# A two-layer retention and gating trunk: constants in one packed load, weight loads held until a stage, value weights in halves, steps one place later

## The reference

```
xn = rmsnorm(h) * norm_g
q, k, v, g_r, u, v_g, g_g = split(xn @ w_in)               # 7 x 1024 columns, 8 heads of 128
o  = retention(rope(q), rope(k) * 128**-0.5, v)            # decayed, chunks of 128, state S per head
o  = groupnorm(o) * silu(g_r)
vn = layernorm(v_g) * ln_g + ln_b
s  = tril(ws[h]) @ vn (per chunk of 128) + bs[h]
m  = u * s * silu(g_g)
h  = h + concat(o, m) @ w_out
```

## Time and profile before

| | |
|---|---|
| median of 3 runs | 1325.68 us (1325.44 to 1326.54) |
| profiled execution | 1327.66 us |
| its span on the slowest core | 1326.1 us (cores: 1317.5 to 1326.1) |
| granted PE clock, mean of the cores | 0.989 to 0.993 |
| PE / PEld busy | 1206.9 / 611.7 us |
| DVE / ACT / POOL busy | 711.7 / 649.4 / 536.1 us |
| moved by DMA | 124.64 MB |

### The profile page before, as it was taken

One profiled execution on the slowest core, in us unless ns is written; L12 is line 12 of the kernel. 1 busy time (PEld: TensorE's weight loads), 2 busy tenths in 40 slices (PEclk: granted clock), 3 DMA queues, 4 the chain that ended last, 5 costly groups with the idle time before them and its releaser, 6 DMA issues.

```text
span 1326.1 us, 23218 instructions; the slowest of 8 cores (1317.5 to 1326.1 us)
## 1 busy us (share of the span) xinstructions
PE 1206.9 (91%) x7524; PEld 611.7 (46%) x7666; DVE 711.7 (54%) x1408; ACT 649.4 (49%) x1053; POOL 536.1 (40%) x528
## 2 busy tenths in 40 slices
PE   0159999999999999998999999999999999999997
PEld 0024445555555555544444444455555555554443
DVE  0024545766677676642233333567777666764333
ACT  1245734665656566553332343465656565563222
POOL 3001002776766677540002100476767667671000
PEclk9979999999999999999999999999999999999999
DMA  9941300523542452388339300054145315425432
GB/s 148 175 140 50 96 19 6 108 46 71 110 84 50 86 118 59 94 150 240 130 123 192 69 1 4 5 109 93 43 92 110 60 48 118 98 75 138 160 129 111
DMA packets 114934, 124.64 MB, mean 94 GB/s; under 512 B 15936, under 2 KB 89920, under 8 KB 113792
## 3 DMA queue, kind: packets, MB, share of 16 engines
q1 hardware_dynamic: 99840, 85.40, 21.8%
q0 software_dynamic: 14976, 37.76, 19.0%
HBM read 126.01 MB, written 34.87 MB: 121 GB/s over the span
## 4 chain that ended last, share of the span: by engine, by line
PE 77%; DVE 9%; SPq 5%; issue 4%; ACT 3%; DMA 1%; POOL 0%; DVEq 0%; ACTq 0%; POOLq 0%
PE ps L656 32%; PE ps L936 18%; PE ps L561 16%; SPq L464 5%; DVE B_k L670 1%; PE ps L895 1%; DVE tt L792 1%; PE ps L790 1%; DVE B_k L669 1%; PE ps L726 1%; PE ps L531 1%; PE ps L810 1%; PE ps L713 1%; PE ps L771 1%; ACT sq L454 1%
## 5 line engine op out<-in xcount | busy, mean ns | idle before, releaser
L454 ACT ACTIVATE B_q<-ps 64x512 f32<-64x512 f32 x128 | 75.7, 591 | 107.4 <-DVE A_q L681 100.9
L454 ACT ACT_TABLE_LOAD x65 | 83.4, 1283 | 37.2 <-DVE tt L792 28.7
L785 POOL TENSOR_TENSOR VO<-og,tt 128x512 bf16<-128x512 f32 x64 | 80.1, 1272 | 23.0 <-ACT tt L454 20.6
L672 POOL TENSOR_TENSOR kT_84<-A_k,B_k 128x512 bf16<-128x512 f32 x32 | 40.7, 1272 | 98.3 <-DVE B_k L670 95.6
L454 ACT ACTIVATE tt<-tt 128x1024 f32<-128x1024 f32 x64 | 67.7, 1057 | 3.6 <-ACT tt L454 0.4
L753 DVE SCALAR_TENSOR_TENSOR S_90<-S_90,ps 128x128 f32<-128x128 f32 x240 | 67.6, 282 | 3.1 <-DVE oS L912 0.4
L887 POOL TENSOR_TENSOR vmask<-eye_137,v_s 16x1024 bf16<-16x1024 f32 x32 | 60.4, 1886 | 18.5 <-PE ps L895 18.1
L621 POOL TENSOR_TENSOR xh_s<-xh_s,lng_s 16x1024 f32<-16x1024 f32 x2 | 4.7, 2336 | 149.3 <-ACT xh_s L454 149.3
L534 DVE TENSOR_TENSOR xnT<-ps,ngT_148 128x1024 bf16<-128x1024 bf16 x16 | 19.4, 1215 | 76.2 <-PE ps L531 39.6
L561 PE MATMUL ps<-wv_103,xnT 128*128 128x512 bf16 x249 | 59.8, 379 | 0.4
L561 PE MATMUL ps<-wv_104,xnT 128*128 128x512 bf16 x253 | 59.7, 379 | 0.2
(11 more groups left out here) (348 smaller groups left out, 3127.5 us busy)
## 6 DMA issues: line engine op xcount, KB each, us to landing
stt_109<-st SPq DMA_DIRECT2D x16, 512.0 KB, 4.1
stt_108<-st SPq DMA_DIRECT2D x16, 512.0 KB, 6.2
ss_out<-stt_108 SPq DMA_DIRECT2D x16, 512.0 KB, 3.3
ss_out<-stt_109 SPq DMA_DIRECT2D x16, 512.0 KB, 7.6
hb_50<-xp SPq DMA_DIRECT2D x8, 512.0 KB, 4.1
hb_51<-xp SPq DMA_DIRECT2D x8, 512.0 KB, 4.4
hb_52<-xp SPq DMA_DIRECT2D x8, 512.0 KB, 4.6
hb_53<-xp SPq DMA_DIRECT2D x8, 512.0 KB, 5.3
```

The costliest lines, as they stand in the source:

```text
L454: P.add("act", lambda e: e.activation(out=out, in_=in_, func=func, **kw), r, w, t_act(n) + (0.2 if "accum_out" in kw else 0), tset=tset)
L672: pool(lambda e: e.tensor_tensor(out=dst[:], in0=A_k[:], in1=B_k[:], op=ALU.add), A_k.k() + B_k.k(), dst.k(), 512)
L785: pool(lambda e: e.tensor_tensor(out=VO[:, h, s], in0=og[:, u.n % 2, :], in1=tt[:, u.n % 2, :], op=ALU.mult), og.k(u.n % 2) + tt.k(u.n % 2 ...
```

## The change

- norm_g, ln_g, ln_b of both layers and w00, b00 are packed by the host into the columns of `c_small` (100 columns instead of 20, one contiguous load); the ten element loads are gone.
- On SP, x chunk 0 is first, then the identity and `c_small`, then the sample rows and x chunks 1 to 3.
- `P.add` takes extra dependencies (`after`). The head weights of blocks 1 and 2 wait for the last value matmul recorded so far (`mark["v"]`).
- Each `wv` is loaded in two halves, and `v_mm` records its eight matmuls as two steps of four, each waiting for its half.
- The scale of a normed chunk goes from ACT to DVE.
- In the output stage of layer 0, `norm_back` comes two chunks behind instead of one, and the `wv` loads of layer 1 are recorded at chunks 5, 7, 9 and 11, each waiting for that chunk's last matmul, instead of all at chunk 2.
- KT is recorded ahead of ONE.
- Guessed durations: SM 0.064 to 0.056, ONE 0.218 to 0.42, `s_proj` 40 x 0.06 to 40 x 0.026, `s_o` 8 x 0.06 to 8 x 0.03.

```diff
-    def add(self, eng, fn, r=(), w=(), dur=0.1, semkey=None, tset=None, nbytes=0):
+    def add(self, eng, fn, r=(), w=(), dur=0.1, semkey=None, tset=None, nbytes=0, after=()):
...
+        for j in after:
+            deps[j] = 2
...
-    w_v = dt_in("w_v", [DEPTH, 4, 128, 8, 512])
+    w_v = dt_in("w_v", [DEPTH, 4, 2, 128, 4, 512])
...
-        ngT = [T("ngT%d" % i, [128, 8], F32) for i in range(2)]
-        lngT = [T("lngT%d" % i, [128, 8], F32) for i in range(2)]
-        lnbT = [T("lnbT%d" % i, [128, 8], F32) for i in range(2)]
-        w00 = T("w00", [128, H], F32)
-        b00 = T("b00", [128, H], F32)
+        sm8 = lambda i: small[:, 20 + 8 * i:28 + 8 * i]
+        ngT, lngT, lnbT, w00, b00 = ([sm8(5 * l + i) for l in range(2)] for i in range(5))
...
-        def w_item(l, item):
+        def w_item(l, item, after=()):
...
-                dma("pool", wv[i][:], w_v[l, i], [], wv[i].k(), wv[i].name, 2097152)
+                for k in range(0, 8, 4):
+                    dma("pool", wv[i][:, k:k + 4, :], w_v[l, i, k // 4], [], wv[i].k((k, k + 4)), (wv[i].name, k), 1048576, after=after)
...
-            act(x_ap, h_ap, AF.Copy, h_k + rst[i].k(), x_k, D, scale=rst[i][0:n, :])
+            dve(lambda e: e.tensor_scalar(out=x_ap, in0=h_ap, scalar1=rst[i][0:n, 0:1], scalar2=None, op0=ALU.mult),
+                h_k + rst[i].k(), x_k, D)
...
-            def mm(e):
-                for k in range(8):
-                    r = e.matmul(ps[:, b, :], xnT[:, k, c * 128:(c + 1) * 128], wv[i][:, k, :], start=(k == 0), stop=(k == 7))
-                return r
-            pe(mm, xnT.k(None, (c * 128, c * 128 + 128)) + wv[i].k(), [bk(b)], 8 * MM)
+            for k0 in range(0, 8, 4):
+                def mm(e, k0=k0):
+                    for k in range(k0, k0 + 4):
+                        r = e.matmul(ps[:, b, :], xnT[:, k, c * 128:(c + 1) * 128], wv[i][:, k, :], start=(k == 0), stop=(k == 7))
+                    return r
+                mark["v"] = pe(mm, xnT.k((k0, k0 + 4), (c * 128, c * 128 + 128)) + wv[i].k((k0, k0 + 4)), [bk(b)], 4 * MM)
...
             if l == 0:
                 dma("sp", h1[c * 128:(c + 1) * 128, :], h[:], h.k(), [("h1", c)], h.name, 524288)
+                if c >= 2:
+                    norm_back(1, c - 2)
                 norm_front(c)
...
         for c in range(4):
             x_load(0, c)
             if c == 0:
+                ld(identf, c_ident)
+                ld(small, c_small, 51200)
                 dma("sp", hs[:], xs_in, [], hs.k(), hs.name, 65536)
-                for l in range(DEPTH):
-                    dma("sp", ngT[l][:], norm_g[l].rearrange("(c p) -> p c", p=128), [], ngT[l].k(), ngT[l].name, 4096,
-                        allow_slow_non_contiguous=True)
...
                     for it in witems[wi:n0]:
-                        w_item(l, it)
+                        w_item(l, it, after=[mark["v"]])
...
+                KT(l, u)
                 if p:
                     ONE(l, p, pp)
-                KT(l, u)
...
-                    if l == 0:
-                        for i in range(4):
-                            w_item(1, ("v", i))
                 if c == 8:
                     s_out(l)
-                if l == 0 and c >= 1:
-                    norm_back(1, c - 1)
+                if l == 0 and c in (5, 7, 9, 11):
+                    w_item(1, ("v", (c - 5) // 2), after=[mark["o"]])
...
             if l == 0:
+                norm_back(1, NCH - 2)
                 norm_back(1, NCH - 1)
```

More of the change, by code:

```diff
@@ L22 @@
 NCORES = 8
+NSMALL = 100
 BLK = 64
@@ L413, in build_nc @@
         eye16 = T("eye16", [NS, NS], F32)
-        small = T("small", [128, 20], F32)
+        small = T("small", [128, NSMALL], F32)
         kinv = lambda h: small[:, h:h + 1]
@@ L450, in pe @@
         def pe(fn, r, w, dur):
-            P.add("pe", fn, r, w, dur)
+            return P.add("pe", fn, r, w, dur)
         def act(out, in_, func, r, w, n, tset=None, **kw):
@@ L461, in pool, with dma @@
             P.add("pool", fn, r, w, t_pool(n))
-        def dma(eng, out, in_, r, w, key, nbytes, **kw):
-            P.add(eng, lambda e: e.dma_start(out=out, in_=in_, **kw), r, w, semkey=key, nbytes=nbytes)
+        def dma(eng, out, in_, r, w, key, nbytes, after=(), **kw):
+            P.add(eng, lambda e: e.dma_start(out=out, in_=in_, **kw), r, w, semkey=key, nbytes=nbytes, after=after)
         def ld(t, src, nbytes=65536, **kw):
@@ L486, in w_item @@
                 t = wsl[slot_of[(l, h, g)]]
-                dma("pool", t[:], w_h[l, h, g], [], t.k(), t.name, 524288)
+                dma("pool", t[:], w_h[l, h, g], [], t.k(), t.name, 524288, after=after)
             else:
@@ L490, in w_item @@
                 t = wo2[wo_of[(l, j)]]
-                dma("pool", t[:], w_o[l, j], [], t.k(), t.name, 1048576)
+                dma("pool", t[:], w_o[l, j], [], t.k(), t.name, 1048576, after=after)
         slot_of, wo_of = {}, {}
@@ L549, in sample_norm @@
             dve(lambda e: e.tensor_tensor(out=sxT[:], in0=pb[:, 0:8 * NS].rearrange("p (k t) -> p k t", k=8),
[L550 to L551 removed]
+                                          in1=ngT[l].unsqueeze(2).to_broadcast([128, 8, NS]), op=ALU.mult),
+                small.k(), sxT.k() + [bk(b)], 128)
+        mark = {}
         vrot = Rot(range(6))
@@ L634, in sample_vg @@
             dve(lambda e: e.tensor_tensor(out=sT_s[:], in0=ps[:, b, 0:8 * NS].rearrange("p (k t) -> p k t", k=8),
[L635 to L638, removed]
+                                          in1=w00[l].unsqueeze(2).to_broadcast([128, 8, NS]), op=ALU.mult),
+                small.k(), sT_s.k() + [bk(b)], 128)
+            dve(lambda e: e.tensor_tensor(out=sT_s[:], in0=sT_s[:], in1=b00[l].unsqueeze(2).to_broadcast([128, 8, NS]),
+                                          op=ALU.add), sT_s.k() + small.k(), sT_s.k(), 128)
         prot = Rot([0, 1, 2])
@@ L789, in ONE @@
             b = brot()
-            pe(lambda e: e.matmul(ps[:, b, :], ones_r[:], sq[:], start=True, stop=True), ones_r.k() + sq.k(), [bk(b)], MM)
+            pe(lambda e: e.matmul(ps[:, b, :], ones_r[:], sq[:], start=True, stop=True), ones_r.k() + sq.k(), [bk(b)], 0.42)
             E = E_h[u.h % 2]
@@ L817, in GM @@
                                                  op0=ALU.mult, op1=ALU.add),
-                lngT[l].k() + Bc[h % 2].k(), s32.k() + [bk(b)], 512)
+                small.k() + Bc[h % 2].k(), s32.k() + [bk(b)], 512)
             g = sgg[u.n % 2]
@@ L839, in w_prep2 @@
                                                  op0=ALU.mult, op1=ALU.add),
-                lnbT[l].k() + gmb[0].k(), Bc[h % 2].k() + [bk(b2)], 128)
+                small.k() + gmb[0].k(), Bc[h % 2].k() + [bk(b2)], 128)
         sstate = {}
@@ L997, in build_nc @@
             if c == 0:
+                ld(identf, c_ident)
+                ld(small, c_small, 51200)
                 dma("sp", hs[:], xs_in, [], hs.k(), hs.name, 65536)
-                for l in range(DEPTH):
-                    dma("sp", ngT[l][:], norm_g[l].rearrange("(c p) -> p c", p=128), [], ngT[l].k(), ngT[l].name, 4096,
-                        allow_slow_non_contiguous=True)
         for i in range(4):
             w_item(0, ("v", i))
-        ld(small, c_small, 10240)
+        P.add("dve", lambda e: e.tensor_copy(identb[:], identf[:]), identf.k(), identb.k())
         ld(maskT, c_maskT)
@@ L1007, in build_nc @@
         for l in range(DEPTH):
[L1008 to L1013, removed]
             if l == 0:
@@ L1163 @@
     w_v = w7[:, :, :, [GCOL["v"], GCOL["vg"]], :].reshape(DEPTH, 8, 128, 2, 2, 512).transpose(0, 3, 4, 2, 1, 5)
-    w_v = w_v.reshape(DEPTH, 4, 128, 8, 512)
+    w_v = w_v.reshape(DEPTH, 4, 128, 2, 4, 512).transpose(0, 1, 3, 2, 4, 5)
     w_o = w_out.reshape(DEPTH, 8, 2, 128, 1024).transpose(0, 1, 3, 2, 4)
-    shared = dict(norm_g=f(norm_g), w_h=f(w_h), w_v=f(w_v), w_o=f(w_o), gm_ws=f(gm_ws), gm_b=f(gm_b), ln_g=f(gm_ln_g),
-                  ln_b=f(gm_ln_b), fin_g=f(final_g), c_small=_C["small"], c_E=_C["E"], c_rope=_C["rope"],
+    cols = lambda a: f(a).reshape(8, 128).T
+    rep = lambda a: np.repeat(f(a).reshape(1, H), 128, axis=0)
+    small = f(np.concatenate([_C["small"]] + [p for l in range(DEPTH) for p in (
+        cols(norm_g[l]), cols(gm_ln_g[l]), cols(gm_ln_b[l]), rep(f(gm_ws)[l, :, 0, 0]), rep(f(gm_b)[l, :, 0]))], axis=1))
+    shared = dict( w_h=f(w_h), w_v=f(w_v), w_o=f(w_o), gm_ws=f(gm_ws), gm_b=f(gm_b), ln_g=f(gm_ln_g),
+                  ln_b=f(gm_ln_b), fin_g=f(final_g), c_small=small, c_E=_C["E"], c_rope=_C["rope"],
                   c_maskT=_C["maskT"], c_ident=_C["ident"], c_eye16=_C["eye16"])
```

17 lines of the change are left out of this document (7 added, 10 removed).

## The result

The changed kernel takes 1271.6 us (median of 4, 1271.55 to 1271.8) against 1325.8 before: a ratio of 0.9591 (0.9574 to 0.9607), 54.2 us less. The forecast was 1257.5, with a range of 1243 to 1277. The opening gave 40 us where 59.5 were forecast; the attention gave 13.8 where 4 were, and for another reason than the one given. The two misses have opposite signs, so the total looks better than its parts.

What follows compares the result with a forecast made beforehand. The opening was taken as bound by transfers, first in order, then in volume. Terms -59.5 - 5.9 + 1 - 4 = -68.4 took the profiled 1327.66 to 1259.3 us; less 2.0 to the median, 1257.5 was stated, range 1243 to 1277.

Steps and rivals of the forecast that it cites:

- the account of the opening: Sign for the start of layer 0's attention: forecast near 148 us; after 165, the explanation of the opening is wrong.
- The opening, forecast -59.5: Start to layer 0's attention: attention starts at 148.2 us instead of 207.7, 59.5 us off.
- By 44 us it can also have done [...] 12.9 us: Opening: by 44 us PE has also done 12.9 us of value matmuls and transposes beyond its earlier progress at 90.6.
- The sum of volumes: Opening: 1.6 us, four value weights 28 and eight x chunks 14.4 give 44 us, taken as PE's dense start.
- The first rival: Opening: x or the clock comes late; 27 us of early work, half at double time, costs 13.5 us; 1271, chance 0.16.
- The fourth rival: Opening: weights' volume alone made x chunk 1 late; it still lands near 33 us; total 1268, chance 0.10.
- Halves, forecast at nothing: Value weights in halves: size costs nothing, starting early up to 3 us once; the skill's rule would add 8 us.
- The output stage, forecast -4.9 net: Output stage of layer 0: 5.9 us gained from the xs stall and slow matmuls, 1 us lost at its end.
- Attention, forecast -4 by KT's cover: Both attention stages: KT ahead of ONE covers its waits, 4 us off, ends 12 off and 4 added.
- at most 17 x 0.23 = 3.9: Attention: KT's four matmuls, 0.23 us, cover ONE's waits in 17 places, at most 3.9 us.
- The new duration estimates move other steps too: Attention: the new guesses can take any part of 26.0 us of idle PE, or add.
- The second rival: Attention: the waits go too, as re-estimated steps are those PE waits at; 20 us instead of 4; 1241.5, chance 0.10.

Runs made afterwards that it cites:

- order and transfers together: Changed kernel with the opening's transfers in order of use and the transposes of x chunks 4 to 7 recorded later in block 0: 1261.8 us, ratio 0.9522.
- the kernel with the still later transposes: Changed kernel with x chunk 4's transposes behind the first v_g chunks too, chunks 5 to 7 after it, transfers unchanged: 1269.2 us, ratio 0.9578.

## Why the prediction was right or wrong

**The total** lies 14 us from the forecast and inside its range, partly by luck. The opening missed 19 us, and 9.8 us of attention that no step of the sum had forecast made up for half of it; without them the time would be 1281. By the prediction's own sign ("If attention starts after 165, the account of the opening is wrong") the account fails on five of the eight cores. (Its last subtraction gives 1257.3, not 1257.5, which changes nothing.)

**The opening, forecast -59.5, came out at -40.1 on the slowest cores.** The step that failed is "By 44 us it can also have done [...] 12.9 us". PE began its dense run at 48.7, not 44: the last x chunk landed at 48.5. The sum of volumes had left out one head weight and ten small loads, which at its own prices are some 3.9 us, as an estimate. By 48.7 PE had done four matmuls, 0.9 us, of the 12.9 credited. From there it needed 118.8 us, where 44 was to be followed by 104.2. Of the 19.3 us missed, 4.7 are the late start, 12.0 the work not done ahead, and 2.6 the run afterwards: PE is idle 2.3 us in it (0.7 before), and one set of transposes, done by that point in the kernel before, was still to do. The weights for the work ahead had landed, the second by about 25 us; what was wrong was to let PE do what the data allowed. It does what the planner wrote down, and the planner gives each queue 150 GB/s of its own, so that for it chunk 4 comes before the second value weight. The trace of before showed the same: PE stood 10.80 us for chunk 4 at 85.97, and the second value weight, in since 2.27 + 19.6 = 21.9, was begun only behind it, at 90.61. Later transposes alone moved the wait to ACT and DVE; order and transfers together brought 9 us back.

**The first rival** named the half clock (it came: 0.50 around the long wait) and x coming late or behind the weights (chunk 4, at 44.48, did), but not PE's order, which makes PE wait for it. Its 1271 is the measured number by accident: its price was half of 27 us at half clock, and in the changed kernel PE works only from 47.89 to about 54 us at it. What half clock can cost is best seen on core 5 of the kernel with the still later transposes: some 4 to 5 us less than on the other cores.

**The cause of the hole** was given as "transfers, first in order, then in volume", as a chain. Undoing showed that either cure alone brings all but 5 to 6 us of what they bring together (25.1): they remove the same wait. The fourth rival (volume alone made chunk 1 late, to land near 33) is out: chunk 1 landed at 17.6, and with the volume back and the elements gone at 18.5; with the volume held and the elements back the issue still lasted 26 us.

**Halves, forecast at nothing** beside up to 3 us once: 4 us gained, with the two recorded steps. The Trainium skill ("DMA: Bandwidth & Descriptors", Bandwidth) advises DMAs of 1 MiB and more; with the fixed cost of some 2 us for each that the same page gives (section "Anatomy of one DMA"), the estimate was 8 us against the halves. Whole weights were 3.9 us slower. The measurement decides here, in a queue that is kept full.

**The held head weights, forecast to cost nothing at the attention's start:** right, value stage and attention join without a wait above 1.5 us. **The scale:** right, 0.75 us on DVE for 1.13 on ACT, and no time.

**The output stage, forecast -4.9 net:** -4.0 on the slowest cores, -5.4 in the mean of the four. The size was right; of the reason, "x chunks compete with value weights" is not shown: issued early again, the weights cost nothing while the transposes came two chunks later.

**Attention, forecast -4 by KT's cover:** -13.8. KT ahead has the other sign (+4). The step "at most 17 x 0.23 = 3.9" counted a cover that was spent already, as KT stood in front of ONE in 14 of the 17 places. The term set aside as "The new duration estimates move other steps too" is the whole gain, 18 us. The second rival had this mechanism ("the re-estimated steps are those PE waits at", 20 us), at a chance of 0.10; KT took 4 of it back. The trace had hints: ONE's successor starts 0.42 us after it (432.49 to 432.91) where the old guess said 0.218, and s_o is shorter than its guess. So, as I read it, the planner wrote down an order in which ONE and SC came before their inputs.

## What to carry to other kernels

Where a planner fixes the order, read its guesses against the trace first: four corrected durations were worth 18 us here, a third of the whole change. When two causes hide the same hole, undo each alone and both together before giving either a price. And data that has landed is no work done: for a fixed order, count from the first step in the queue whose input is late, on every engine.

## What was not expected of the hardware

How long a load takes depended on what else was in flight, more than the forecast allowed. With DMA share 0.99 to 1.05 between 10 and 40 us, x chunk 1 took 14.7 us to land beside the weights and chunk 4 some 33.8 (10.51 to 44.3), chunk 0 only 3.9. Holding three weights back brought chunk 3 to 18.4 from 4.24 + 22.6 = 26.8 us, and chunk 4 came no later for it: ACT began on it at 44.69, against 44.48. And in one execution, on one program, one core kept its clock at 1.00 through the value stage while it fell twice on the other seven.
